# Hybrid decoder layer in f32: one h sum from two f32 tiles, small columns behind x's scaling, w_o's second operand in halves, the last rows' residual in PSUM

## The chip, the cores and the metric

The kernel runs on one core of one Trainium2 chip. The metric is the time of one execution on the device in microseconds (us); lower is better. A core has TensorE (matmuls; PE in the profile, PEld for its weight loads), VectorE (DVE), ScalarE (ACT), GpSimd (POOL) and SyncE (SP), which issues most DMAs. They run side by side and meet through semaphores. Matmul results land in PSUM, everything else lies in SBUF.

## The reference

One decoder layer on 512 tokens of width 1024, all in f32. Cut to what matters:

```
h = rmsnorm(x, attn_norm_g)
u_b, u_c, u_x, q, k, v, g_conv, g_attn = split(h @ w_in)
y_conv = (u_b * short_conv(u_c * u_x, conv_w)) @ w_conv_out
y_attn = sliding_window_attention(q, k, v, sinks, rel_bias) @ w_attn_out
x = x + (sigmoid(g_conv) * y_conv + sigmoid(g_attn) * y_attn) @ w_o
h2 = rmsnorm(x, mlp_norm_g)
x = x + square(relu(h2 @ w_up)) @ w_down
return rmsnorm(x, final_norm_g)
```

## The kernel before

**Precision.** Every f32 operand is split into a high part (ScalarE rounds it to fp32r) and a low part (VectorE subtracts the high part from the f32 value). A product is three passes of matmuls, called kinds in the code: high by high, low by high, high by low. So each product needs a ScalarE copy before its first pass and a VectorE subtraction before each of the others.

**Fast products.** The q projection and the 13 stages GC, GA, CO, AO, WO and eight stages of w_up and w_down use a Strassen scheme of seven products of 2 x 2 blocks: M1, N2, M6, M5, M7, M3, N4, in this order. Their left operands are corners of the activations or sums of corners (S1 to S4), their right ones weight blocks or sums of weight blocks (T1 to T4). Results of several products add up in the same PSUM region, and ScalarE copies or VectorE sums take them out between products.

**Front.** SP loads x in four blocks of 128 rows between halves of the first q weights. For each block ScalarE takes the sum of squares and a root (`root(b)`, lines 1221 to 1228), VectorE takes its reciprocal and scales the block (`scale_x`, lines 1749 to 1754), and TensorE transposes it (`x_transposes`). Behind the second block's transposes come four idle transposes and product M1. The gain columns `pcol` come from a transpose of `prow`; VectorE copies them out of PSUM (line 1797). With them VectorE and ScalarE take each transposed tile into `h`, split in high and low (`tile_high`, `tile_low`). ScalarE also writes the second half's tiles unsplit into `qa` (`tile_whole`, counted by `wide`). These are the corners A21 and A22; the corner A11 exists only as high and low parts in `h`.

**h sums of the q product.** VectorE makes S3 = A11 - A21 (`h_s3`, two steps), S2 = -A22 - S3 (`h_s2`), S1 = A11 + S2 (`h_s1`, two steps: A11's high part, then its low part) and S4 = A12 + S2 (`h_s4`, two steps). `hs_step` counts the steps. `sum_high` and `sum_low` split each sum; they feed M7, M6, M5 and M3 of the q product. In VectorE's order, `h_s1` stands directly ahead of `q_low_part(M6)`, the low part of M6's weights, which M6's third pass waits for.

**Mixer.** Behind the q product come k and v's heads and four blocks of conv strips (c, x, b) with attention between them. The first scores (TensorE, lines 811 and 812) need `qs`, which VectorE finishes only when the table `bias` has landed (line 2057 waits for it, and `stage_queries` follows).

**Stage WO.** Here `mixed` is the left operand. Product M1 has transposes of the last corner of `mixed` between its matmuls (`mixed_corner_21`); `s_high(WO, N2)` copies that corner's high part straight from PSUM (line 1472), `s_low` the low part. N2 adds to a copy of M1's result (`seed_out`, counted by `o_seeded`), one half of rows each.

**End.** In the last stage `res` holds the residual. VectorE drains products into it (`drain`, `drain_last_m3`, `drain_n4`). N4 runs row block by row block (`by_blocks`), three passes each; `drain_n4(12, 1)` adds the last one, rows 3, columns 0 to 511. ScalarE sums the squares of each row block in two halves, takes the root (`root_of`), VectorE the reciprocal (`factor`) and scales one half (`scale_late`), ScalarE the other (`scale_early`); SP and ScalarE store.

Of the kernel before, what the change touches and what calls it, by code (L numbers as in the profile page):

```python
# [9 lines left out]
ALU = mybir.AluOpType  # L10
# [201 lines left out]
def build(nc, x, attn_norm_g, w_in, conv_w, w_conv_out, attn_sinks, rel_bias, w_attn_out, w_o,  # L212
          mlp_norm_g, w_up, w_down, final_norm_g, out):
    ctx = ExitStack()
    with ctx:
# [132 lines left out]
        def sem(name):  # L348
            return ctx.enter_context(nc.semaphore(name))
# [41 lines left out]
        m_hi, m_lo, t_sum = sem("m_hi"), sem("m_lo"), sem("t_sum")  # L391
        t1_base, t1_in, t3_base, t3_in = sem("t1_base"), sem("t1_in"), sem("t3_base"), sem("t3_in")
        copied, half_copied = sem("copied"), sem("half_copied")
        o_seeded = sem("o_seeded")
        summed, relu_done = sem("summed"), sem("relu_done")
        squared, s_sum, s_hi, s_lo = sem("squared"), sem("s_sum"), sem("s_hi"), sem("s_lo")
        ao_sum = sem("ao_sum")
        prod, drained, gfin_in = sem("prod"), sem("drained"), sem("gfin_in")
        passed = sem("passed")
        root_done, root3_part, root3_done = sem("root_done"), sem("root3_part"), sem("root3_done")  # L400
        ss3_ready, fin_step = sem("ss3_ready"), sem("fin_step")
# [367 lines left out]
        def _(pe):  # L769
# [282 lines left out]
            def product(s, i, fresh, between={}):  # L1052

                n, thi, tlo = weight_parts(s, i)
                if s < CO:
                    shi, slo = gate_part(i)
                else:
                    shi, slo = s_hi_tile[slot_of(s, i)], s_lo_tile[slot_of(s, i)]
                parts = [(shi, thi), (slo, thi), (shi, tlo)]
                order = [(b, kind) for b in range(2) for kind in range(3)] if by_blocks(s, i) else \  # L1060
                    [(b, kind) for kind in range(3) for b in range(2)]
                if seeded(s) and i == N2:
                    order = [(0, 0), (0, 1), (1, 0), (1, 1), (0, 2), (1, 2)]
                for at_, (b, kind) in enumerate(order):
                    if n == 0 and kind == 0:
                        pe.wait_ge(free_dve[b], frees("D", b, S_OUT - 1))
                    if s == WO and i == N2 and kind == 0:
                        pe.wait_ge(o_seeded, b + 1)
                    if seeded(s) and i == N2 and kind == 0:
                        pe.wait_ge(copied, copied_no(s, 1)) if b else pe.wait_ge(half_copied, s)  # L1070
                    if b == 0:
                        if kind == 0:
                            pe.wait_ge(m_hi, n + 1)
                            if s >= CO:
                                pe.wait_ge(s_hi, part_no(s, i) + 1)
                            elif i in HS:
                                pe.wait_ge(hs_in[HS.index(i)], 32)
                        elif kind == 1:
                            if s >= CO:
                                pe.wait_ge(s_lo, part_no(s, i) + 1)  # L1080
                        else:
                            pe.wait_ge(m_lo, n + 1)
                    a_, w = parts[kind]
                    for k in range(4):
                        last = mm(pair[region(s, i)][:, b, :], a_[:, k, b * P:(b + 1) * P], w[:, k, :],  # L1085
                                  start=(fresh and kind == 0 and k == 0), stop=(kind == 2 and k == 3),
                                  skip_group_check=True)
                    if kind == 2:
                        last.then_inc(prod, 1)
                    if at_ in between:  # L1090
                        between[at_]()
# [25 lines left out]
            for s in range(STAGES):  # L1117
# [65 lines left out]
                pe.wait_ge(drained, base_ + 3 + more)  # L1183
                product(s, M3, False)
                pe.wait_ge(drained, base_ + 4 + more)
                if s == WO:
                    pe.wait_ge(h2_raw, 4)
                    residual_transposes(1, 1, 0)
# [4 lines left out]
        def _(act):  # L1193
# [84 lines left out]
            root(1)  # L1278
            q_high_half(M1, 0)
            q_high_half(M1, 1)  # L1280
            act.wait_ge(par_ready, 1)
            for k in range(4, 8):
                act.wait_ge(h_ready, k - 3)
                tile_high(0, k, k)
            root(2)
            q_high_half(N2, 0)
            q_high_half(N2, 1)
            root(3)
# [10 lines left out]

            def sum_high(i):  # L1300

                act.wait_ge(hs_step, {M7: 2, M6: 3, M5: 5, M3: 7}[i])
                k = HS.index(i)
                a(hs_hi[k][:, :, :], hs_sum[k][:, :, :], ACT.Copy).then_inc(hs_split, 1)

            def q_copy(i, j, of, done, scale=1.0):

                act.wait_ge(q_prod, 2 * Q_ORDER.index(of) + 2)
                if i:
                    act.wait_ge(hs_step, 3)  # L1310
                a(four_of(qa, i, j), four(Q_REGION.get(of, 3))[:, :, :], ACT.Copy, scale=scale).then_inc(done, 1)

            q_copy(0, 0, M1, q_c11_base)
# [141 lines left out]
            def s_high(s, i):  # L1455

                at_ = part_no(s, i)
                if i in (M1, N2, N4):
                    if s == CO:
                        for j in range(2):  # L1460
                            act.wait_ge(free_dve[j], frees("D", j, S_OUT - 1))
                    elif s == AO:
                        act.wait_ge(pv_out, QUADS * TB)
                    elif s == WO:
                        act.wait_ge(mix_t, 4) if i == N2 else act.wait_ge(mix_ready, {M1: 2, N4: 1}[i])
                    else:
                        act.wait_ge(squared, 4 * ((s - 6) // 2) + {M1: 1, N4: 2, N2: 3}[i])
                else:
                    act.wait_ge(sums(s), sums_before(s) + {M7: 1, M6: 2, M5: 3, M3: 4}[i])
                wait_used(act, *part_before(s, i))  # L1470
                src = four(0) if (s, i) == (WO, N2) else part_source(s, i)
                a(s_hi_tile[slot_of(s, i)][:, :, :], src[:, :, :], ACT.Copy).then_inc(s_hi, 1)  # L1472

            def seed(s):

# [130 lines left out]
            def square(s, at_):  # L1606
# [3 lines left out]
                    act.wait_ge(s_lo, part_no(s - 1, N4) + 1)  # L1610
                a(a_part(s, i, j), src[:, :, :], ACT.Square).then_inc(squared, 1)

            def sum_squares(b, ch, part):
                a(tz[:, 0, 0:512], res[:, b, 512 * ch:512 * ch + 512], ACT.Square,
                  accum_out=ss3[:, part, b:b + 1]).then_inc(ss3_ready, 1)

            def early_squares(b):
# [87 lines left out]
            act.wait_ge(root3_part, 1)  # L1705

            def root_of(b):
                act.wait_ge(drained, drained_before(STAGES - 1) + 6 + b)
                act.wait_ge(ss3_ready, TB + b)
                sum_squares(b, 1 - early(b), 1)  # L1710
                act.wait_ge(ss3_ready, TB + b + 1)
                a(rms3[:, 1, b:b + 1], ss3[:, 1, b:b + 1], ACT.Sqrt, bias=rms3[:, 0, b:b + 1],
                  scale=1.0 / D).then_inc(root3_done, 1)
# [23 lines left out]
        def _(dve):  # L1737
# [55 lines left out]
                    tile_low(1, at_, LATE_TILES[at_])  # L1793

            scale_x(0)
            dve.wait_ge(par_t, 1)
            v.tensor_copy(pcol[:, :], bank[KT - 1][:, T - 5 * KT:T]).then_inc(par_ready, 1)
            scale_x(1)
            dve.wait_ge(par_ready, 1)
            for k in range(4):  # L1800
                tile_high(k)
# [34 lines left out]
                                       op0=ALU.mult, op1=ALU.subtract).then_inc(hs_step, 1)  # L1836

            def h_s1():
                step_done(3)
                v.tensor_tensor(hs_sum[2][:, :, :], h_part(0, 0, 0), hs_sum[1][:, :, :], ALU.add).then_inc(hs_step, 1)  # L1840
                step_done(4)
                v.tensor_tensor(hs_sum[2][:, :, :], hs_sum[2][:, :, :], h_part(1, 0, 0), ALU.add).then_inc(hs_step, 1)

            def h_s4():
                step_done(3)
                v.tensor_tensor(hs_sum[3][:, :, :], h_part(0, 0, 1), hs_sum[1][:, :, :], ALU.add).then_inc(hs_step, 1)
                step_done(6)
                v.tensor_tensor(hs_sum[3][:, :, :], hs_sum[3][:, :, :], h_part(1, 0, 1), ALU.add).then_inc(hs_step, 1)

            def sum_low(i):  # L1850
# [266 lines left out]
            def drain_n4(s, b):  # L2117
# [4 lines left out]
                r = res[:, 2 + b, 0:512]  # L2122
                v.tensor_tensor(r, r, pair[region(s, N4)][:, b, :], ALU.add).then_inc(drained, 1)

            def drain_last_m3(b):

                s = STAGES - 1
                dve.wait_ge(prod, 14 * s + 2 * M3 + b + 1)
                dve.wait_ge(drained, drained_before(s) + 5 + b)
                r = res[:, b, 512:D]  # L2130
                v.tensor_tensor(r, r, pair[region(s, M3)][:, b, :], ALU.add).then_inc(drained, 1)
# [239 lines left out]
            def scale_late(b):  # L2371

                dve.wait_ge(fin_step, b + 1)
                ch = 1 - early(b)
                r = res[:, b, 512 * ch:512 * ch + 512]
                v.scalar_tensor_tensor(out=r, in0=r, scalar=rms3[:, 2, b:b + 1], in1=gfin[:, 512 * ch:512 * ch + 512],
                                       op0=ALU.mult, op1=ALU.mult).then_inc(out_late, 1)

            for s in range(WO + 1, STAGES, 2):
# [42 lines left out]
                low_part(s + 1, M3)  # L2422
                drain(s + 1, 3 + more, 1, 1, M7, ALU.subtract)
                if last:
                    drain_last_m3(0)
                s_low(s + 1, N4)
                low_part(s + 1, N4)
# [13 lines left out]
            factor(1)  # L2441
            scale_late(1)
            gain(3)
            drain_n4(STAGES - 1, 1)
            factor(2)
            scale_late(2)
            dve.wait_ge(gained_late, 1)
# [25 lines left out]
```

## Time and profile before

| | us |
|---|---|
| median of 3 runs | 751.18 (751.17 to 751.3) |
| the profiled execution | 751.2 |
| its span | 749.5 |
| TensorE busy | 741.1 (99%), 4198 matmuls |
| VectorE busy | 656.3 (88%) |
| ScalarE busy | 430.0 (57%) |
| GpSimd busy | 85.5 (11%) |
| granted TensorE clock, mean | 0.999 |

The span is what the profiler's rows cover; the 1.7 us around it belong to the time too. A row of the timeline is one instruction or a run of like ones: start, time, engine, line, operation, written tile <- read tiles, shapes, count, and in brackets how long the engine had been idle and what ended that. Matmuls overlap, and their ends are modelled, so two products are compared by starts.

### The profile page before, as it was taken

To read this page: it belongs to the slowest core of one execution; us is meant where nothing else is said; L and a number is where in the kernel's file an instruction comes from. 1 tells how busy PE (TensorE), PEld (TensorE's weight loads), DVE (VectorE), ACT (ScalarE), POOL (GpSimd) and SP (SyncE) were. 2 spreads that over 40 slices of the span, in tenths; PEclk is the share of its full clock that TensorE was granted. 3 is DMA by queue.
4 is the path that set the end of the run, shared out by engine and by line. 5 is a ranking of instruction groups with operands and counts; after the bars stand their busy time and mean duration, and the time that the engine had idled before them with its cause. 6 is when DMAs were issued, how large, how long until landed. Compare 5 with 4: busy or idle time off the path is not lost.

```text
span 749.5 us, 10670 instructions
## 1 busy us (share of the span) xinstructions
PE 741.1 (99%) x4198; PEld 650.7 (87%) x4198; DVE 656.3 (88%) x759; ACT 430.0 (57%) x551; POOL 85.5 (11%) x120
## 2 busy tenths in 40 slices
PE   9999999999999999999999999999999999999996
PEld 8899888888888888888888899889988999899985
DVE  5996788989899686989999999998799879986997
ACT  6773555453644557564658776654565455545555
POOL 1520000111122101010100101010101010100102
PEclk9999999999999999999999999999999999999999
DMA  9899313161247987777767747677677767686703
GB/s 319 200 316 321 112 57 113 57 164 61 84 127 236 305 232 196 195 225 193 255 169 177 213 124 208 179 201 193 169 191 202 174 171 219 168 215 180 197 1 113
DMA packets 69443, 135.45 MB, mean 181 GB/s; under 512 B 2636, under 2 KB 18068, under 8 KB 69396
## 3 DMA queue, kind: packets, MB, share of 16 engines
q1 hardware_dynamic: 48848, 85.23, 33.6%
q0 software_dynamic: 20336, 49.30, 30.3%
q8 instruction: 32, 0.52, 0.3%
q10 hardware_dynamic: 212, 0.28, 0.1%
q14 instruction: 15, 0.12, 0.1%
HBM read 128.48 MB, written 6.32 MB: 180 GB/s over the span
## 4 chain that ended last, share of the span: by engine, by line
PE 94%; DVE 4%; ACT 1%; issue 1%; POOL 0%; POOLq 0%; DVEq 0%; ACTq 0%
PE pair L1085 45%; PE pair L1044 22%; PE pair L790 6%; PE pair L792 6%; PE pair L791 6%; PE pair L911 3%; PE pair L837 2%; PE pair L812 1%; PE pair L811 1%; PE pair L821 1%; PE pair L859 1%; DVE h L1788 1%; PE pair L1007 0%; PE pair L995 0%; DVE wgt L1745 0%
## 5 line engine op out<-in xcount | busy, mean ns | idle before, releaser
L1390 ACT ACTIVATE high<-home_raw 128x2048 fp32r<-128x2048 f32 x91 | 174.3, 1916 | 148.4 <-PE pair L1085 102.9
L2014 DVE TENSOR_TENSOR home_lo<-home_raw,high 128x2048 fp32r<-128x2048 f32 x91 | 208.4, 2290 | 34.6 <-ACT high L1390 34.1
L1085 PE MATMUL pair<-high,s_hi_tile 128*128 128x512 f32 x440 | 110.3, 391 | 0.3 <-ACT s_hi_tile L1472 0.3
L1085 PE MATMUL pair<-high,s_lo_tile 128*128 128x512 f32 x440 | 109.9, 390 | 0.0
L1085 PE MATMUL pair<-home_lo,s_hi_tile 128*128 128x512 f32 x440 | 109.5, 389 | 0.0
L1085 PEld LDWEIGHTS pair<-home_lo,s_hi_tile 128*128 128x128 f32 x440 | 82.5, 188 | 17.1
L1085 PEld LDWEIGHTS pair<-high,s_lo_tile 128*128 128x128 f32 x440 | 82.4, 188 | 17.1
L1085 PEld LDWEIGHTS pair<-high,s_hi_tile 128*128 128x128 f32 x440 | 81.8, 188 | 17.7 <-issue 0.7
L790 PE MATMUL pair<-h,wgt 128*128 128x512 f32 x192 | 76.5, 399 | 0.0
L792 PE MATMUL pair<-h,wgt 128*128 128x512 f32 x192 | 75.0, 390 | 0.0
L791 PE MATMUL pair<-h,wgt 128*128 128x512 f32 x192 | 74.9, 390 | 0.0
L1044 PE MATMUL pair<-h_hi,home_lo 128*128 128x256 f32 x448 | 58.4, 283 | 0.0
L1044 PE MATMUL pair<-h_lo,high 128*128 128x256 f32 x448 | 58.4, 283 | 0.0
L1044 PE MATMUL pair<-h_hi,high 128*128 128x256 f32 x448 | 58.3, 283 | 0.0
L1044 PEld LDWEIGHTS pair<-h_hi,high 128*128 128x128 f32 x448 | 56.0, 192 | 0.3
L1044 PEld LDWEIGHTS pair<-h_hi,home_lo 128*128 128x128 f32 x448 | 55.8, 192 | 0.0
L1044 PEld LDWEIGHTS pair<-h_lo,high 128*128 128x128 f32 x448 | 55.8, 192 | 0.0
L792 PEld LDWEIGHTS pair<-h,wgt 128*128 128x128 f32 x192 | 36.0, 188 | 7.9
L791 PEld LDWEIGHTS pair<-h,wgt 128*128 128x128 f32 x192 | 36.2, 188 | 6.6
L790 PEld LDWEIGHTS pair<-h,wgt 128*128 128x128 f32 x192 | 36.1, 188 | 6.7
L1362 ACT ACTIVATE pr<-pr,neg_m 128x128 f32<-128x128 f32 x64 | 24.8, 390 | 26.1 <-DVE pr L1930 22.8
L1745 DVE TENSOR_TENSOR wgt<-raw,wgt 128x1024 fp32r<-128x1024 f32 x26 | 30.8, 1221 | 6.5 <-ACT wgt L1211 6.4
(228 smaller groups left out, 1129.5 us busy)
## 6 DMA issues: line engine op xcount, KB each, us to landing
home_raw<-in_w_up SPq DMA_DIRECT2D x16, 1024.0 KB, 5.3
home_raw<-in_w_down SPq DMA_DIRECT2D x16, 1024.0 KB, 5.1
raw<-in_w_in SPq DMA_DIRECT2D x26, 512.0 KB, 4.8
home_raw<-in_w_up POOLq DMA_DIRECT2D x12, 1024.0 KB, 8.2
home_raw<-in_w_down POOLq DMA_DIRECT2D x12, 1024.0 KB, 8.4
home_raw<-in_w_in POOLq DMA_DIRECT2D x7, 1024.0 KB, 8.6
home_raw<-in_w_in SPq DMA_DIRECT2D x7, 1024.0 KB, 7.1
home_raw<-in_w_conv_out SPq DMA_DIRECT2D x4, 1024.0 KB, 5.2
```

What stands on the lines that cost most here:

```text
L790: mm(bank[j][:, :], wh, rhs[:, 0, k, :], start=(k == 0), stop=False)
L791: mm(bank[j][:, :], wh, rhs[:, 1, k, :], start=False, stop=False)
L792: last = mm(bank[j][:, :], wl, rhs[:, 0, k, :], start=False, stop=(k == KT - 1))
L811: mm(acc, q, khi[:, kg, keys], start=True, stop=False)
L837: last = mm(bank[B_PV][:, :], vs[:, kb, kg, :, :].rearrange("p a d -> p (a d)"), pt[:, part, kb, :], start=(e == 0), stop=(e == len(steps) ...
L911: last = mm(acc[:, f, :], w[:, k, f * P:(f + 1) * P], a_[:, k, :], start=(i in (M1, N2, M5) and kind == 0 and k == 0 and f % 2 == 0), stop ...
L1044: last = mm(acc[:, f, :], w[:, k, f * P:(f + 1) * P], a_[:, k, :], start=(fresh and kind == 0 and k == 0 and f % 2 == 0), stop=(kind == 2 ...
L1085: last = mm(pair[region(s, i)][:, b, :], a_[:, k, b * P:(b + 1) * P], w[:, k, :], start=(fresh and kind == 0 and k == 0), stop=(kind == 2 ...
L1362: a(v, v, ACT.Exp, bias=neg_m[:, qd % 2, i:i + 1], accum_out=den[:, qd % 2, i:i + 1])
L1390: a(high[n % 2][:, :], home_raw[home_of(s, name)][:, :], ACT.Copy).then_inc(m_hi, 1)
L1745: v.tensor_tensor(w[:, 1, 1024 * e:1024 * e + 1024], raw[raw_slot(2 * s1 + e)][:, :], f32(w[:, 0, 1024 * e:1024 * e + 1024]), ALU.subtract ...
L2014: v.tensor_tensor(home_lo[home][:, :], home_raw[home][:, :], f32(high[n % 2][:, :]), ALU.subtract).then_inc(m_lo, 1)
```

## The change

- The h sum S1 is made in one step, A21 - A22, from the two unsplit tiles in `qa`; the steps that follow count one less, and the q copies that overwrite these tiles wait for it.
- VectorE copies `pcol` behind the second block's scaling rather than ahead of it. ScalarE takes the third block's root ahead of its four tile copies rather than behind them.
- In stage WO the high part of N2's second operand is copied in two halves; TensorE waits for the first (`o_first`) ahead of the product and for the second ahead of its third matmul.
- In the last stage VectorE adds the residual of rows 3, columns 0 to 511, into the PSUM bank ahead of N4 (`add_residual`, new, behind the drain of M7); N4's second row block adds up on it. Its drain is dropped, and ScalarE's squares and VectorE's final scaling of these rows read PSUM. TensorE waits for the new sum (`rested`) ahead of N4.

The diff, cut:

```diff
@@ product
-                            if s >= CO:
+                            if s == WO and i == N2:
+                                pe.wait_ge(o_first, 1)
+                            elif s >= CO:
                                 pe.wait_ge(s_hi, part_no(s, i) + 1)
...
                     for k in range(4):
+                        if s == WO and i == N2 and (b, kind, k) == (0, 0, 2):
+                            pe.wait_ge(s_hi, part_no(s, i) + 1)
@@ TensorE, stage order
                 pe.wait_ge(drained, base_ + 4 + more)
+                if s == STAGES - 1:
+                    pe.wait_ge(rested, 1)
@@ ScalarE, front
             q_high_half(M1, 1)
+            root(2)
             act.wait_ge(par_ready, 1)
             for k in range(4, 8):
                 act.wait_ge(h_ready, k - 3)
                 tile_high(0, k, k)
-            root(2)
@@ sum_high, q_copy
-                act.wait_ge(hs_step, {M7: 2, M6: 3, M5: 5, M3: 7}[i])
+                act.wait_ge(hs_step, {M7: 2, M6: 3, M5: 4, M3: 6}[i])
...
                 if i:
-                    act.wait_ge(hs_step, 3)
+                    act.wait_ge(hs_step, 4)
@@ s_high
-                src = four(0) if (s, i) == (WO, N2) else part_source(s, i)
-                a(s_hi_tile[slot_of(s, i)][:, :, :], src[:, :, :], ACT.Copy).then_inc(s_hi, 1)
+                src, first = four(0) if (s, i) == (WO, N2) else part_source(s, i), 0
+                if (s, i) == (WO, N2):
+                    first = 2
+                    a(s_hi_tile[slot_of(s, i)][:, 0:2, :], src[:, 0:2, :], ACT.Copy).then_inc(o_first, 1)
+                a(s_hi_tile[slot_of(s, i)][:, first:4, :], src[:, first:4, :], ACT.Copy).then_inc(s_hi, 1)
@@ sum_squares, root_of
+            def last_rows(b, ch):
+
+                return pair[region(STAGES - 1, N4)][:, 1, :] if (b, ch) == (3, 0) else res[:, b, 512 * ch:512 * ch + 512]
...
-                a(tz[:, 0, 0:512], res[:, b, 512 * ch:512 * ch + 512], ACT.Square,
+                src = last_rows(b, ch) if part else res[:, b, 512 * ch:512 * ch + 512]
+                a(tz[:, 0, 0:512], src, ACT.Square,
...
-                act.wait_ge(drained, drained_before(STAGES - 1) + 6 + b)
+                if b < 3:
+                    act.wait_ge(drained, drained_before(STAGES - 1) + 6 + b)
+                else:
+                    wait_used(act, STAGES - 1, N4)
@@ VectorE, front
             scale_x(0)
+            scale_x(1)
             dve.wait_ge(par_t, 1)
             v.tensor_copy(pcol[:, :], bank[KT - 1][:, T - 5 * KT:T]).then_inc(par_ready, 1)
-            scale_x(1)
@@ h_s1, h_s4
             def h_s1():
-                step_done(3)
-                v.tensor_tensor(hs_sum[2][:, :, :], h_part(0, 0, 0), hs_sum[1][:, :, :], ALU.add).then_inc(hs_step, 1)
-                step_done(4)
-                v.tensor_tensor(hs_sum[2][:, :, :], hs_sum[2][:, :, :], h_part(1, 0, 0), ALU.add).then_inc(hs_step, 1)
+                v.tensor_tensor(hs_sum[2][:, :, :], four_of(qa, 1, 0), four_of(qa, 1, 1), ALU.subtract).then_inc(hs_step, 1)
...
-                step_done(6)
+                step_done(5)
@@ VectorE, end
+            def add_residual():
+
+                s = STAGES - 1
+                dve.wait_ge(drained, drained_before(s) + 5)
+                acc = pair[region(s, N4)][:, 1, :]
+                v.tensor_tensor(acc, acc, res[:, 3, 0:512], ALU.add).then_inc(rested, 1)
...
-                v.scalar_tensor_tensor(out=r, in0=r, scalar=rms3[:, 2, b:b + 1], in1=gfin[:, 512 * ch:512 * ch + 512],
+                src = pair[region(STAGES - 1, N4)][:, 1, :] if b == 3 else r
+                v.scalar_tensor_tensor(out=r, in0=src, scalar=rms3[:, 2, b:b + 1], in1=gfin[:, 512 * ch:512 * ch + 512],
...
                 if last:
+                    add_residual()
                     drain_last_m3(0)
...
             gain(3)
-            drain_n4(STAGES - 1, 1)
             factor(2)
```

## Rows read from the trace of the kernel before

**Rows 1.** The page's first part: busy us, share, instructions of each engine.

```profile
PE 741.1 (99%) x4198; PEld 650.7 (87%) x4198; DVE 656.3 (88%) x759; ACT 430.0 (57%) x551; POOL 85.5 (11%) x120
```

**Rows 2.** The list of waits, TensorE alone: waiter <- releaser: total us, times, longest.

```profile
PE pair L911 <- DVE q_lo L1768: 0.2, 1, 0.2
```

**Rows 3.** Timeline, second block of x: start, us, engine, line, operation [idle before].

```profile
7.12 0.29 ACT L1227 ACTIVATE rms<-ssq,eps 128x1 f32<-128x1 f32 x1
...
7.46 0.20 DVE L1797 COPY pcol<-pair 128x40 f32<-128x40 f32 x1 [0.42 <-PE pair L864]
...
9.12 1.66 DVE L1776 TENSOR_SCALAR h<-pair,pcol 128x256 fp32r<-128x256 f32 x4 [0.61 <-PE pair L851]
```

**Rows 4.** Timeline, third and fourth block; then x's loads there, issue and landing.

```profile
11.27 1.60 ACT L1264 ACTIVATE h<-pair,pcol 128x256 fp32r<-128x256 f32 x4 [0.76 <-issue]
...
13.93 0.30 ACT L1227 ACTIVATE rms<-ssq,eps 128x1 f32<-128x1 f32 x1
...
17.52 0.17 DVE L1752 RECIPROCAL rms<-rms 128x1 f32<-128x1 f32 x1 [0.47 <-ACT rms L1227]
...
L542 SPq DMA_DIRECT2D xn<-in_x x2: 442/537/632, 2.8 to 3.5; - x2
...
DMA to landing us min/median/max: 7.8/8.1/8.4
```

**Rows 5.** Timeline, products M6, M5 and M7 of q and VectorE's h sum.

```profile
34.41 2.08 PE L911 MATMUL pair<-hs_hi,q_hi 128*128 128x256 f32 x16
...
35.14 1.22 DVE L1842 TENSOR_TENSOR hs_sum<-hs_sum,h 128x1024 f32<-128x1024 f32 x1
36.28 2.28 DVE L1768 TENSOR_TENSOR q_lo<-q_raw,q_hi 128x2048 fp32r<-128x2048 f32 x1
...
37.80 2.01 ACT L1241 ACTIVATE q_hi<-q_raw 128x1024 fp32r<-128x1024 f32 x2 [0.34 <-DMA q_raw<-in_w_in]
...
40.63 2.08 PE L911 MATMUL pair<-hs_hi,q_hi 128*128 128x256 f32 x16
...
46.39 2.08 PE L911 MATMUL pair<-hs_hi,q_hi 128*128 128x256 f32 x16
```

**Rows 6.** A stretch (busy us per engine; last: clock, DMA share, GB/s); timeline, first scores.

```profile
32.00:72.00 40.00, 39.78 (x291) 37.80 (x290) 33.21 (x27) 21.30 (x21) 6.41 (x10) 1.00 1.06 325
...
68.48 0.56 DVE L2057 TENSOR_TENSOR vdif<-vnat 128x384 f32<-128x384 f32 x1 [6.10 <-DMA bias<-bias_rows]
...
69.07 2.47 DVE L1903 TENSOR_TENSOR qs<-qa,qs 64x1024 fp32r<-64x1024 f32 x2
...
72.05 0.19 PEld L811 LDWEIGHTS pair<-khi,qs 128*128 128x128 f32 x1
```

**Rows 7.** Timeline, stage WO from M1's end to N2's third pass.

```profile
391.56 1.03 ACT L1472 ACTIVATE s_hi_tile<-pair 128x1024 fp32r<-128x1024 f32 x1 [0.29 <-PE pair L1007]
...
392.62 1.23 DVE L2070 TENSOR_TENSOR s_lo_tile<-pair,s_hi_tile 128x1024 fp32r<-128x1024 f32 x1 [0.18 <-ACT s_hi_tile L1472]
392.70 1.69 PEld L1085 LDWEIGHTS pair<-high,s_hi_tile 128*128 128x128 f32 x8 [0.68 <-issue]
...
393.76 2.28 DVE L2014 TENSOR_TENSOR home_lo<-home_raw,high 128x2048 fp32r<-128x2048 f32 x1
...
396.25 1.77 PEld L1085 LDWEIGHTS pair<-home_lo,s_hi_tile 128*128 128x128 f32 x8
396.47 1.98 PE L1085 MATMUL pair<-home_lo,s_hi_tile 128*128 128x512 f32 x8
```

**Rows 8.** Timeline of VectorE in the last stage's end.

```profile
735.19 0.69 DVE L2131 TENSOR_TENSOR res<-res,pair 128x512 f32<-128x512 f32 x1 [0.50 <-PE pair L1085]
...
742.80 0.68 DVE L2369 TENSOR_TENSOR res<-res,gfin 128x512 f32<-128x512 f32 x1
743.40 0.68 DVE L2123 TENSOR_TENSOR res<-res,pair 128x512 f32<-128x512 f32 x1
...
745.25 0.15 DVE L2362 RECIPROCAL rms<-rms 128x1 f32<-128x1 f32 x1
```

More of the change, by code:

```diff
@@ L393, in build @@
         copied, half_copied = sem("copied"), sem("half_copied")
-        o_seeded = sem("o_seeded")
+        o_seeded, o_first = sem("o_seeded"), sem("o_first")
         summed, relu_done = sem("summed"), sem("relu_done")
@@ L397, in build @@
         ao_sum = sem("ao_sum")
-        prod, drained, gfin_in = sem("prod"), sem("drained"), sem("gfin_in")
+        prod, drained, rested, gfin_in = sem("prod"), sem("drained"), sem("rested"), sem("gfin_in")
         passed = sem("passed")
```

## The prediction, made before the change was run

> **What bounds the kernel now.** I read the page first: the TensorE row is busy for 741.1 of 749.5 us [rows 1], so time is won only where TensorE stands still, has not begun, or has already ended. The list of waits by engine, TensorE alone, has three entries: the start, one on q_lo of 0.2 us [rows 2], and one on s_hi_tile, met again in edit 3. That list counts from a matmul's modelled end, so I measured both stalls again from starts in the timeline. The reader is to look for three places: the front up to 72 us, where VectorE and ScalarE feed TensorE just in time; the passage inside stage WO at 392 us; and the last 6 us, where no matmul runs and VectorE and ScalarE work by turns. The edits lie in these places, two in the first, one each in the others. From 72 to 735 us the kernel runs at TensorE's pace: loads wait for its progress (`wait_used`), so a gain in front should shift all behind it, unless something there stands at a fixed time. One thing does: the table `bias`.
>
> **Edit 1, the small columns behind x's scaling.** ScalarE's root of the second block ends at 7.41, but VectorE copies pcol first (7.46, 0.20 us) [rows 3] and begins the scaling's reciprocal behind it, some 0.08 before the copy's end (such overlaps below), at 7.58. Without the copy ahead it can start at about 7.46: 0.12 us earlier. The scaling, x's second transposes, four idle transposes and product M1 follow in a row, so TensorE has the 0.12. The copy moves into VectorE's wait of 0.61 us for these transposes [rows 3]; without that cover it would cost its 0.20 again.
> root(2) goes ahead of the four tile copies. ScalarE is idle for 0.76 us before them, from 10.51 to 11.27 [rows 4]. x's third block is issued at 2.8 and takes at least 7.8 us [rows 4], so it lands at 10.6, and the root, which in before stands behind the copies (from 12.78 to 14.23), then runs from 10.65 to 12.1. The price: tiles 4 to 7 come 0.8 us later, where nobody is near: VectorE takes them up behind the third block's scaling, TensorE with product N2. root(3) ends up to 0.45 earlier, and VectorE's wait of 0.47 for it at 17.52 [rows 4] goes. But what TensorE waits for there, the transposes of x's fourth block, isn't in its list at all, so it is below 0.1: I take 0.06 (0 to 0.1). Sum of edit 1: 0.18 us (0.12 to 0.22). If the q copies behind find their load not yet landed, the 0.06 goes and the 0.12 stays.
>
> **Edit 2, one h sum.** Two sums of 1.22 us become one, whose inputs VectorE has already waited for. Product M6 takes 40.63 - 34.41 = 6.22 us from its first matmul to M5's first; M5, with the same 48 matmuls, takes 46.39 - 40.63 = 5.76 [rows 5]: the stall on q_lo is 0.46. q_lo ends at 38.56; without one sum (1.22 and a gap of 0.04) at 37.3, with edit 1 at 37.1, and TensorE asks for it 0.46 before it gets it now, at 38.1. The stall goes whole: 0.46. Next late: M5's q_hi, which waits for a transfer and is ready at 39.81 [rows 5], independent of the edit; M5 begins at 39.99 and needs its second half a quarter pass later. The q copies now wait for four steps instead of three; the fourth ends before 35.2, the first copy that heeds it follows M5, so that wait is free.
>
> **Where the front's gain can be lost.** The two edits bring TensorE to the first scores 0.64 us earlier. There it needs qs: VectorE starts vdif at 68.48, when the table `bias` has landed, and ends the two halves of qs at 71.54; the scores' first load is at 72.05 [rows 6]. With 0.04 for the signal the slack is 0.47, not 0.64. The table's load stands behind q's products on SP's queue and is issued earlier too; does it land earlier? From 32 to 72 us the DMA share is 1.06 at 325 GB/s [rows 6], that is, the engines are full: I take the same landing, 0.01 off for what comes with it, hence 0.46. Bounds: 0.66 if the table moves along, 0.2 if it lands 0.27 later, since POOL's T3 block, which starts when the h sums are stored, comes earlier as well and shares the engines.
> The Trainium skill, DMA: Bandwidth & Descriptors, section Issuing engines are not separate DMA queues, says that transfers of all issuing engines run on the same 16 engines and interleave, whoever started them. By that rule the early issue is worth nothing and the front gives 0.46; with a table that moves with its issue, 0.64. No row of before shows it by itself.
>
> **Edit 3, w_o's second operand in halves.** ScalarE copies s_hi in 1.03 us from 391.56. TensorE's load for N2 comes at 392.70, behind an idle 0.68 [rows 7]: that is the stall. In the steady flow a load runs 0.22 ahead of its matmul (396.25 and 396.47), so a part of a load's lateness doesn't show; I take 0.11 of the 0.22. With a first half of about 0.6 us, done at 392.16, the load comes at 392.25 and 0.45 or more of the stall goes. But two halves end about 0.08 later than one copy (a fixed part twice). VectorE's s_low waits for the second (392.62, 1.23 us) and low_part follows without a gap (393.76, 2.28 us) to 396.05; N2's third pass loads at 396.25 [rows 7]. That slack of 0.20, less 0.05 for the signal and the 0.08, plus the hidden 0.11, is all that TensorE keeps: 0.18 us. seed_out(1) and ScalarE's work behind it are 0.08 later, which M6, the next product, doesn't see: its loads come after N2's third pass. Bounds: 0 (the halves cost 0.25 more) and 0.3.
>
> **Edit 4, the residual in PSUM.** Behind the last matmul VectorE adds the last rows at 743.40 (0.68 us); the reciprocal for these rows is at 745.25 [rows 8]. The add goes, and ScalarE squares PSUM directly. VectorE starts an instruction 0.60 after such an add (743.40 behind 742.80), so its queue is 0.60 shorter. ScalarE's part, 745.25 - 744.08 = 1.17 us with both signals, then starts with the last matmul's end (743.34) and is done at 744.5: it binds no longer, VectorE's queue does. Against this, add_residual is new in that queue, ahead of drain_last_m3(0), which waited 0.50 for TensorE until 735.19 [rows 8]. It can start at 734.73, takes 0.69 like the drain of the same size, and the drain may follow at 735.33: 0.14 late, with s_low, low_part and all of VectorE's tail. N4's third pass waits for that low_part, so TensorE ends up to 0.14 later, 744.65 for ScalarE's part, still ahead of VectorE. The reciprocal comes at 745.25 - 0.60 + 0.14 = 744.79: 0.46 us, and the stores behind it with it. TensorE's new wait on `rested` (done at 735.4) is for N4, behind the whole of M3: free, 0.14 if not. Bounds: 0.25 (the add from and to PSUM takes 0.9) and 0.6 (it hides in the 0.50).
> The final scaling now reads PSUM. A sum with one operand in PSUM (743.40) and one from SBUF alone (742.80) both take 0.68 us [rows 8]: no difference, as I take it. The Trainium skill, VectorE: DVE Perf Modes, section The TRN2 errata, gives a PSUM source 62 cycles more; by that estimate, 0.065 us, edit 4 would give 0.40.
>
> **Sum.** 0.46 + 0.18 + 0.46 = 1.10 us. The profiled execution took 751.2 us, of which 749.5 are its span; the median of the runs is 751.18, so the sum needs no correction: 750.1 us. All bounds on the good side give 0.66 + 0.3 + 0.6 = 1.56: 749.6; on the bad side 0.2 + 0 + 0.25 = 0.45: 750.75.
>
> **Rivals.** (a) The table moves with its issue, the halves cost nothing and the new add hides: about 1.5 us, 749.6. For it: VectorE's work ahead of these transfers is earlier by up to 1.4 us. Against: the full DMA engines.
> (b) Only the end gains: the front is given back at the scores or the next weights, and stage WO's gain behind low_part: 0.4 us, 750.8. For it: slacks of 0.47 and 0.20.
> (c) Slower: the table lands much later, because the T3 block of 1 MB gets ahead of it. Each microsecond by which it lands later takes one from the 1.1; it decides from 69.6 on. At 325 GB/s the block is 3.2 us; that half of it is served first would be 1.6 later, 751.7. Against: both are in the queues as it is, and the work up to the landing stays the same.
> (d) The PSUM sum doesn't spare its instruction, as when N4 waits for `rested`: bounded in edit 4.
>
> **How the numbers follow.** A measurement of this kernel can tell about 0.2%, 1.5 us, from no change. Forecast (749.75 to 750.65): 0.66; (a) 0.17; (b) 0.12; (c) 0.05. Faster by over 0.2% (under 749.68) is (a) and a little of the forecast's good end, 0.18; slower by over 0.2% lies past (c)'s price, 0.02; within is the rest, 0.80. The range takes the forecast, (a)'s near half and (b): 749.5 to 750.85.
>
> **What would show it.** Right: no TensorE wait on q_lo; M5's first matmul at 39.99; vdif still at about 68.5 and the scores' first load near 71.6, not 71.4; N2's third pass bound by low_part; the last reciprocal directly behind the other blocks' work on VectorE. Wrong: vdif at 67.9 (a) or past 69 (c), a TensorE wait on `rested`, or a new wait between 72 and 735 us that takes back what the front gave.

## The result and the profile after

The changed kernel takes 754.52 us (median of 7 executions, 752.93 to 756.97) where the kernel before takes 751.18 (750.95 to 751.5): a ratio of 1.0041, 95% interval 1.0031 to 1.0052. The forecast was 750.1, its range ended at 750.85. So the change makes the kernel slower, by more than the 0.2% that such a measurement can tell, and it makes the seven executions differ by 4 us where the seven of the kernel before differed by half a microsecond (in larger sets of that kernel single ones took up to 752.92). The profiled execution took 755.13 us, of which 753.4 are its span: 3.9 more than before.

The page's first part, the row that answers to [rows 1], and behind it two rows from the list of waits of TensorE in the first 80 us (waiter <- releaser: total us, times, longest), which answers to [rows 2]:

```profile
PE 742.4 (99%) x4198; PEld 651.5 (86%) x4198; DVE 655.2 (87%) x758; ACT 429.9 (57%) x552; POOL 85.0 (11%) x120
```

```profile
PE pair L911 <- ACT hs_hi L1310: 2.3, 1, 2.3
...
PE pair L911 <- ACT q_hi L1247: 0.9, 1, 0.9
```

The wait on q_lo is gone, as forecast. These two have come, both at q's products (L911). The timeline of M6 and M5, which answers to [rows 5], shows that the front's gain arrived and where it was lost (start, us, engine, line, operation, [idle before <- releaser]):

```profile
34.13 2.08 PE L911 MATMUL pair<-hs_hi,q_hi 128*128 128x256 f32 x16
36.05 2.08 PE L911 MATMUL pair<-hs_lo,q_hi 128*128 128x256 f32 x16
37.97 2.08 PE L911 MATMUL pair<-hs_hi,q_lo 128*128 128x256 f32 x16
40.92 1.34 PE L911 MATMUL pair<-hs_hi,q_hi 128*128 128x256 f32 x9 [0.87 <-ACT q_hi L1247]
...
52.73 0.63 PE L952 MATMUL pair<-ident,ty 128*128 128x128 f32 x4
...
55.61 1.69 PE L911 MATMUL pair<-hs_hi,q_hi 128*128 128x256 f32 x11 [2.26 <-ACT hs_hi L1310]
```

M6's third pass starts at 37.97, 0.65 earlier than the 38.62 of the trace before: the 0.64 of edits 1 and 2 is there in this pair of executions. Then M5 begins at 40.92, where it began at 40.63 [rows 5], and M3 at 55.61, where it began at 52.50. The rows of the trace before for these comparisons, and of ScalarE's copy of M3's load:

```profile
38.62 2.17 PE L911 MATMUL pair<-hs_hi,q_lo 128*128 128x256 f32 x16 [0.22 <-DVE q_lo L1768]
...
47.51 1.90 ACT L1256 ACTIVATE q_hi<-q_raw 128x2048 fp32r<-128x2048 f32 x1
...
52.50 2.15 PE L911 MATMUL pair<-hs_hi,q_hi 128*128 128x256 f32 x16
```

What ScalarE waited for ahead of these, and what GpSimd and SyncE's queue issued there, stands in the timeline of the changed kernel:

```profile
37.33 1.32 POOL L673 DMA_DIRECT2D q_raw<-in_w_in  x1 [2.21 <-DVE q_lo L1785]
38.46 0.75 POOL L699 DMA_DIRECT2D h_sums<-hs_hi  x1
39.00 0.74 POOL L699 DMA_DIRECT2D h_sums<-hs_lo  x1
39.81 2.00 ACT L1247 ACTIVATE q_hi<-q_raw 128x1024 fp32r<-128x1024 f32 x2 [3.89 <-DMA q_raw<-in_w_in]
39.88 0.37 SPq L549 DMA_DIRECT2D q_raw<-in_w_in  x1
...
52.61 1.91 ACT L1262 ACTIVATE q_hi<-q_raw 128x2048 fp32r<-128x2048 f32 x1 [4.61 <-DMA q_raw<-in_w_in]
54.43 1.04 ACT L1310 ACTIVATE hs_hi<-hs_sum 128x1024 fp32r<-128x1024 f32 x1
```

L673 at 37.33 is GpSimd's accumulating transfer of 1 MB for N4 (`add_q(N4)`), which waits for q_lo of M6. L549 at 39.88 is SyncE's load of 1 MB for M3 (`load_q(M3)`, semaphore q_b22), which waits for the landing of M5's accumulation (q_t1_in). In the trace before they stand the other way round:

```profile
37.87 0.37 SPq L549 DMA_DIRECT2D q_raw<-in_w_in  x1
38.86 1.32 POOL L673 DMA_DIRECT2D q_raw<-in_w_in  x1 [3.48 <-DVE q_lo L1768]
```

Before, M3's load took 7.1 us from issue to landing (45.0) and ScalarE took it up without a wait at 47.51. After, it took 12.7 (52.6); ScalarE stood idle for 4.61 us for it, and hs_hi, which TensorE names, is only the next instruction in ScalarE's queue. The chain of work that ended last (start, us, what) says it in three lines: M5's base load, M5's accumulation, M3's load, one behind the other.

```profile
19.39 10.49 DMA q_raw<-in_w_in
30.17 9.61 DMA q_raw<-in_w_in
39.88 12.71 DMA q_raw<-in_w_in
```

The third part of the loss is the clock. Stretches of 4 us of the changed kernel (busy us by engine; the last three columns are granted clock, DMA share, GB/s):

```profile
48.00:52.00 4.00, 4.00 (x36) 4.00 (x35) 3.92 (x6) 0.00 (x1) 0.00 (x0) 1.00 1.04 416
52.00:56.00 4.00, 1.71 (x13) 1.33 (x13) 1.08 (x2) 3.39 (x3) 0.00 (x0) 1.00 1.04 393
56.00:60.00 4.00, 4.00 (x24) 4.00 (x23) 3.97 (x3) 3.27 (x3) 1.06 (x2) 0.61 1.10 363
60.00:64.00 4.00, 4.00 (x35) 4.00 (x33) 3.79 (x4) 0.00 (x0) 0.00 (x0) 0.97 1.07 398
```

From 56.9 to 60.3, beginning 1.3 us after TensorE took up work again, the matmuls of M3 follow each other every 0.213 us instead of 0.120: the engine was granted 1.2 GHz instead of 2.4, which makes the mean of the third stretch 0.61.

The whole account, from the start of the same matmul in both traces (after minus before): -0.65 at M6's third pass, +0.29 at M5's first matmul, +0.58 at the transposes in front of M3, +3.11 at M3's first matmul, +4.60 where the clock is full again, +4.59 at the first scores, and +3.92 at VectorE's last reciprocal. So the front lost 0.94 before M5, 0.29 up to the transposes, 2.53 before M3 and 1.49 to the clock, and the edits behind it gave back 0.67.

### The profile page after: what moved, and what is told of

The parts are those of the page before. It is cut to its first block, busy times and chain, and to the rows that moved or that the text cites. A ratio compares the mean times of both kernels' runs of the same rounds, so it can differ in the third digit from the quotient of the medians.

```text
span 753.4 us, 10670 instructions
## 1 busy us (share of the span) xinstructions
PE 742.4 (99%) x4198; PEld 651.5 (86%) x4198; DVE 655.2 (87%) x758; ACT 429.9 (57%) x552; POOL 85.0 (11%) x120
## 4 chain that ended last, share of the span: by engine, by line
PE 87%; DMA 5%; DVE 4%; issue 2%; ACT 1%; ACTq 0%; SPq 0%; DVEq 0%
PE pair L1089 41%; PE pair L1044 20%; PE pair L790 6%; PE pair L792 6%; PE pair L791 6%; DMA q_raw<-in_w_in 4%; PE pair L911 3%; PE pair L837 2%; DVE home_lo L2028 2%; PE pair L812 1%; PE pair L811 1%; PE pair L821 1%; DVE res L2129 1%; ACT high L1396 1%; DMA xn<-in_x 0%
```

## Experiments

Three theories were set against each other. A: q's transfers. It has two forms: A1, M3's load is passed by N4's accumulation, because edit 2 brings GpSimd's issue forward; A2, M5's accumulation is late by itself, because edit 1 brings its base load forward. B: the order of instructions on ScalarE and VectorE. C: the end edits. The four parts come first, each against the kernel before.

**Edits 1 and 2 alone** (the diff's hunks for `root(2)`, `scale_x`/`pcol`, `h_s1` and its step numbers).

> Only edits 1 and 2 (x's scaling and root order, one h sum); stage WO and the tail as before. Theory A (q's transfers): the whole loss sits here, in M5's wait for q_t1_in (0.9 us) and M3's wait for q_b22 (2.5 us) with the low clock behind it (1.5 us); so 753.5 to 757.5 us, that is 0.6 to 0.7 above the full change, with the same run-to-run spread of some 4 us, and the load of q_b22 landing at about 52 instead of 45. Theory B (the order on ScalarE and VectorE, not the transfers, makes the waits): the waits on hs_hi and q_hi stand with the loads landing long before the copies begin. Theory C (the end edits cost it): 750.5 to 751.0 and no new wait.

754.08 us (750.52 to 756.3); ratio 1.0031, 1.0014 to 1.0047. In its trace N4's accumulation is issued at 37.43, M3's load at 39.43; it lands 13.0 us later, and TensorE waits 2.5 us before M3. The copies begin when their load lands, within 0.1 us. C and B fall. Two details of A's expectation were missed: the wait before M5 was 0.3 us instead of 0.9, and the time isn't 0.6 to 0.7 above the full change's but 0.44 below it, in a kernel whose executions differ by 5.8 us. Three of its 12 executions took 750.5 to 750.65, some 0.65 less than before, the forecast's gain of the front; no trace shows one of them.

**Edit 1 alone.**

> Only edit 1 (pcol's copy behind x's scaling, root(2) ahead of the tile copies). N4's accumulation is issued behind q_lo of M6, so with edit 1 alone still at about 38.6, after or with q_b22's load (37.9 or later). Theory A1 (N4's accumulation passing q_b22's load is the cause): q_b22 lands by 47 and M3 doesn't wait; 751.0 to 751.6. Theory A2 (the base load of M5, issued 0.27 us earlier against M7's accumulation, is the cause): q_t1_base lands near 29.9, q_t1_in past 38.7, q_b22 after 48, TensorE waits for both; 752.5 or more, with a wide spread.

751.35 us (750.81 to 753.28), ratio 1.0006, 0.9997 to 1.0015: no loss that can be told, and no gain. N4's accumulation goes out at 38.70, M3's load at 39.10, and it lands 6.4 us later. q_t1_base landed at 29.53 and q_t1_in at 39.01, but TensorE didn't wait for it. By the median, A2's 752.5 didn't come. But five of the 11 executions took 752.67 to 753.28, where five of the 35 of the kernel before took 752.18 or more; no trace shows one of them, so what they waited for stays open.

**Edit 2 alone.**

> Only edit 2 (h_s1 in one sum). q_lo of M6 ends 1.26 earlier, so N4's accumulation is issued at about 37.6 instead of 38.87. Theory A1: q_b22 lands late (49 or more), TensorE waits 1 to 3 us before M3 and its clock falls behind it; 752.5 to 756. Theory A2: q_t1_base lands at 29.1 as before, q_t1_in near 37.8, q_b22 near 45; 750.7 to 751.0, the forecast's gain of 0.46.

754.91 us (750.65 to 757.51), ratio 1.004, 1.0022 to 1.0058. The loss comes with this edit alone, the one that only takes work away.

```profile
38.32 1.32 POOL L673 DMA_DIRECT2D q_raw<-in_w_in  x1 [2.21 <-DVE q_lo L1768]
39.65 0.37 SPq L549 DMA_DIRECT2D q_raw<-in_w_in  x1
```

In these rows of its timeline SyncE issues in the moment in which GpSimd's issue ends, and M3's load already takes 12.3 us to its landing. TensorE waits 1.9 us before M3.

**Edits 3 and 4 alone.**

> Only edits 3 and 4 (w_o's operand in halves, residual in PSUM); the front as before. Theory of the forecast: 0.18 + 0.46 = 0.64 faster, 750.5 us, spread as of before (0.5). The rival that the halves or the PSUM sum cost something: 751.2 or more. By the changed kernel's trace (shift of TensorE's last matmul against the shift before stage WO, and of the last reciprocal): 0.68.

750.67 us against 751.25, ratio 0.9995, 0.9987 to 1.0004: the 0.58 lies near the 0.64 of the sum, in an interval that takes in no change as well. Nothing is lost there.

The next two test the order itself, from both sides.

**The full change, N4's accumulation held back.**

```
 pool.wait_ge(q_low, 5)
+pool.wait_ge(q_t1_in, 16)
 add_q(N4, 1, 0, q_t4_in)
```

> The full change, with one wait more: GpSimd issues N4's accumulation only when q_t1_in has landed, as SyncE does with q_b22's load, so that SyncE's short issue (0.37 us) comes ahead of GpSimd's (1.3 us). Theory A1 (the order of these two transfers is the whole loss): q_b22 lands 6 to 8 us after its issue, at 45 to 47, no wait before M3, the front keeps its 0.46 to 0.66 and the kernel takes 750.0 to 750.4, the time that was forecast. Theory A2 (M5's accumulation is late by itself, since its base load is issued earlier beside M7's): q_t1_in at 38.5 to 39.8 all the same, 0.3 to 0.9 us of wait before M5 stay; 750.5 to 751.3, and more where the clock falls behind that wait.

750.23 us (749.8 to 751.13) against 751.26: ratio 0.9988, 0.9979 to 0.9997. One wait more on an engine that is 11% busy takes 4.3 us off the changed kernel's time, and the sum of the forecast, 750.1, is met within 0.13. Rows of its timeline, and then the last line of the view of L549, its time from issue to landing:

```profile
39.41 0.37 SPq L549 DMA_DIRECT2D q_raw<-in_w_in  x1
39.89 1.32 POOL L673 DMA_DIRECT2D q_raw<-in_w_in  x1 [4.55 <-DMA q_raw<-in_w_in]
...
40.45 0.74 PE L912 MATMUL pair<-hs_hi,q_hi 128*128 128x256 f32 x4 [0.19 <-ACT q_hi L1248]
```

```profile
DMA to landing us min/median/max: 5.6/5.6/5.6
```

M3's load lands after 5.6 us, at 45.0 as before, and N4's accumulation, now behind it, takes 14.1 (54.0) without a stall of TensorE. A wait before M5 is left (0.2 in this execution, which took 750.64), since q_t1_in landed at 39.32: A2's landing came, the time that it asked for didn't.

**The same without edit 1.**

> As the kernel before it, but with edit 1 undone (edits 2, 3, 4 and N4's accumulation held for q_t1_in). Theory A1: 750.2 to 750.5, as the one with edit 1 or up to 0.2 above. Theory A2: the base load of M5 is issued at 19.7 again and q_t1_in lands at 37.8 to 38.2; no wait before M5, so faster than with edit 1, 750.1 to 750.3 against 750.5 to 751.3.

750.28 us (749.99 to 751.3), ratio 0.9988, 0.9979 to 0.9997. A2 wanted M5's wait to go: it didn't, q_t1_in landed at 39.96 in the profiled execution (751.3, the slowest of the 11) and TensorE waited 0.7. So M5's accumulation can be late without edit 1, and edit 1 brings nothing here that can be told (0.05).

**The kernel before, with the two transfers in the reverse order.**

```
...
 add_q(N4, 1, 0, q_t4_in)
+pool.wait_ge(bias_out, 16)
+g.memset(ext[:, 0:1], NEG).then_inc(n4_out, 1)
...
+sp.wait_ge(n4_out, 1)
 load_q(M3, 1, 1, q_b22)
```

> The kernel before, every instruction as it was, but q_b22's load is issued only when GpSimd has issued N4's accumulation (a one-column fill on GpSimd behind the issue tells SyncE): at about 40.3 instead of 37.87. Theory A1: q_b22 lands at 50 to 53, though its issue is only 2.4 us later; TensorE waits 1 to 3 us before M3, 752.5 to 756, with a wide spread. Rival (the load is late by its issue alone, 45.0 + 2.4 = 47.4; ScalarE takes it up at 47.5): no wait, 751.2.

756.21 us (755.81 to 757.91), ratio 1.0066, 1.0052 to 1.008. None of the edits is in this kernel, and it has the loss, in every execution. First two rows of its timeline, then the time of L549 from issue to landing, then the first line of the list of waits. The profiled execution is the slowest of the five (757.91).

```profile
39.19 1.32 POOL L674 DMA_DIRECT2D q_raw<-in_w_in  x1 [3.47 <-DVE q_lo L1771]
40.63 0.37 SPq L549 DMA_DIRECT2D q_raw<-in_w_in  x1
```

```profile
DMA to landing us min/median/max: 13.4/13.4/13.4
```

```profile
PE pair L914 <- ACT hs_hi L1307: 4.0, 1, 4.0
```

The load is issued 2.8 us later than before and lands 9.0 us later (54.04 against 45.01). A1 stands, though it came out dearer than expected (a wait of 4.0 us for 1 to 3, and a time 0.2 over the 756); the rival's 47.4 doesn't.

**Edit 3 alone.**

> Only edit 3 (w_o's second operand in halves). The forecast: 0.18, so 751.0; by the changed kernel's trace N2's third pass begins 0.32 earlier, so up to 0.32, 750.85, if nothing gives it back behind. Rival: given back in the next products, 751.2. Edit 4 is the difference to the run with both (750.67).

751.11 us against 751.26, ratio 1.0, 0.9991 to 1.0009. The 0.15 lies near the forecast's 0.18, but no run resolves it.

**The full change, M3's load set free from q_t1_in.** The other way to put it ahead of N4's accumulation.

```
-sp.wait_ge(q_t1_in, 16)
 load_q(M3, 1, 1, q_b22)
```

> The full change, but SyncE doesn't wait for q_t1_in before q_b22's load: it is issued behind bias_rows, at about 30.1 instead of 39.9, at the same time as M5's accumulation (30.2, 1.3 us of issue on GpSimd). Theory A1 (whichever of two 1 MB transfers is issued first is served first): q_b22 lands by 36, M3 never waits, but M5's accumulation comes behind it: q_t1_in at 41.5 to 43 instead of 39.8, TensorE waits 1.5 to 3 us before M5; 751.5 to 754. Rival (the idle time of the DMA engines between 28 and 32 us, where their share is 0.34, takes the load in): q_t1_in at 39.8 or little later, at most 1 us of wait before M5; 750.0 to 750.8, as good as holding N4's accumulation back.

752.35 us (750.18 to 754.17), ratio 1.0015, 1.0006 to 1.0024. Again the transfer issued first is served first, only that the victim is now M5's accumulation: M3's load (29.70) lands in 5.5 us, M5's accumulation, issued 0.11 behind it, takes 11.5 instead of 9.6 and lands at 41.27 (expected: 41.5 to 43). Its timeline, then the first line of its list of waits:

```profile
29.70 0.37 SPq L549 DMA_DIRECT2D q_raw<-in_w_in  x1
29.81 1.29 POOL L672 DMA_DIRECT2D q_raw<-in_w_in  x1 [3.48 <-DMA q_raw<-in_w_in]
```

```profile
PE pair L910 <- ACT q_hi L1246: 2.3, 1, 2.3
```

The share of 0.34 that the DMA engines show between 28 and 32 us in the changed kernel didn't take 1 MB more in without making the accumulation behind it late.

All ten traces with both transfers at this place, sorted by the time that M3's load took:

| kernel | N4's issue, start to end | M3's load issued | its time to landing |
|---|---|---|---|
| full, N4 held, no edit 1 | 40.53 to 41.85 | 40.05 | 5.4 |
| full, N4 held | 39.89 to 41.21 | 39.41 | 5.6 |
| edit 1 | 38.70 to 40.02 | 39.10 | 6.4 |
| edit 3 | 38.74 to 40.07 | 38.83 | 6.9 |
| before | 38.86 to 40.19 | 37.87 | 7.1 |
| edits 3 and 4 | 38.93 to 40.25 | 38.04 | 7.2 |
| edit 2 | 38.32 to 39.65 | 39.65 | 12.3 |
| full change | 37.33 to 38.65 | 39.88 | 12.7 |
| edits 1 and 2 | 37.43 to 38.76 | 39.43 | 13.0 |
| before, reversed | 39.19 to 40.51 | 40.63 | 13.4 |

In the first six rows SyncE's load is issued before GpSimd's issue of 1.32 us has ended, in the last four when it has. Where between the two the border lies isn't measured: the latest load of the first group went out 0.40 us after the start of GpSimd's issue, the earliest of the second 1.33 us after it.

## Why the prediction was wrong, point by point

**Edit 2, "Next late: M5's q_hi, which waits for a transfer and is ready at 39.81, independent of the edit".** This is the step that failed, twice. First, M5's q_hi is not the dearest of what comes late next. q_lo of M6, which the edit moves forward by 1.26 us, has a second reader beside TensorE: GpSimd waits for it with `add_q(N4)`. The forecast followed the earlier q_lo to TensorE alone. One look at who waits for q_lo would have shown 1 MB set off 1.3 us earlier, which in the trace before was issued only 1.0 us behind M3's load. The term that this cost, a late M3 at 2.53 us and the lower clock behind it at 1.49, isn't in the sum at all. Second, "independent of the edit" took a landing of one execution for a fixed time. In the traces of the five kernels without edit 2's sum q_t1_in landed at 37.78, 37.95, 38.74, 39.01 and 39.01. The trace before is the earliest of these; the slack of a microsecond that hid the others was just what the 0.64 of the front was to consume. In the six with it, N4 held back or not, q_t1_in landed at 39.32 to 41.27. The loss needs both: with N4's issue 1.3 us earlier (37.6 to 38.9) and M3's load still at 37.87, the load would have been issued before GpSimd's issue had ended, as in the table's first group; in the three kernels with edit 2 and the loss it was issued only at 39.43 to 39.88, behind q_t1_in. What makes that transfer late is told only for the run in which M3's load was set free. For the rest it stays open: already q_t3_base, issued and landed before any instruction that edit 2 touches, came at 17.88 to 18.40 in the six and at 17.14 to 17.85 in the five.

**"The stall goes whole: 0.46", edit 1's 0.18.** Right up to 37.97 (0.65 for 0.64). Of the 0.65, 0.28 is there at M6's first matmul (34.13 for 34.41) and 0.37 comes inside M6. The second part is firm: from M6's first matmul to its third pass it is 3.83 or 3.84 us in all six traces with edit 2 and 4.16 to 4.21 in the five without, and with edit 2 alone M6 takes 5.75 us instead of 6.22. The first is edit 1's 0.18 mixed with what two executions differ by: M6 begins at 34.13 to 34.35 in the five traces with edit 1 and at 34.34 to 35.13 in the six without. Whether edit 1's part reaches the end wasn't resolved by any run.

**"Where the front's gain can be lost".** The right question at the wrong transfer. The forecast looked for a transfer that is passed by another and took the table `bias`, the one thing whose landing stood in TensorE's way at 72 us. The table wasn't it: it landed earlier, not later, with vdif at 66.73 in the changed kernel and at 67.57 with N4 held, against 68.48 [rows 6].

```profile
66.73 0.56 DVE L2071 TENSOR_TENSOR vdif<-vnat 128x384 f32<-128x384 f32 x1
...
76.64 0.19 PEld L811 LDWEIGHTS pair<-khi,qs 128*128 128x128 f32 x1
```

So the "same landing" was wrong too, on the good side; the cut from 0.64 to 0.46 wasn't put to the test by the changed kernel, whose first scores come at 76.64 for other reasons. The Trainium skill, DMA: Bandwidth & Descriptors, section Issuing engines are not separate DMA queues, has transfers of all engines interleave on the same 16. The traces agree once packets of both queues are moving (205 of GpSimd's queue and 197 of SyncE's from 45 to 48 us in the changed kernel); before that, the transfer issued later waits for its first packet, and so M3's load takes 5.4 to 7.2 us when it is issued first and 12.3 to 13.4 when GpSimd's megabyte has been issued, while N4's accumulation takes 10.0 to 11.7 in front and 12.3 to 14.2 behind (packets in the last section).

**Rival (c)**, with a chance of 0.05, had the mechanism, a transfer that gets ahead of another, and the sign. It was tied to `bias` and priced at 1.6 us by bandwidth alone. It left out that a late operand costs TensorE twice: 2.5 us of wait, and 1.49 at the lower clock behind it. In other traces a wait of 1.9 us (edit 2), 2.3 (M3's load set free) or 4.0 (the reversed order) was followed by stretches of 4 us at 0.70, 0.78 and 0.50 as well; in that of edits 1 and 2, a wait of 2.5 us was followed by none, with 1.00 from 52 to 64 us. So the clock's part comes or doesn't. The mean clock of the changed kernel's executions fits this as one source of their spread (0.999 in the two fastest, 752.93 and 753.40; 0.995 in two of the three slowest, 755.13 and 756.97); the landing itself is likely another, but only one of the seven has a trace.

**The signs.** None of the signs of being wrong that the prediction lists names this place: it looked for a new wait from 72 us on, and both came before 56. One of its signs of being right does, M5's first matmul at 39.99, and that one failed (40.92). Its sign for a faster kernel, vdif at 67.9, was more than met (66.73) in a slower one.

**Edit 3.** The mechanism is right. The rows that answer to [rows 7]:

```profile
396.16 0.60 ACT L1480 ACTIVATE s_hi_tile<-pair 128x512 fp32r<-128x512 f32 x1 [0.29 <-PE pair L1007]
396.65 0.59 ACT L1481 ACTIVATE s_hi_tile<-pair 128x512 fp32r<-128x512 f32 x1
396.87 0.77 PEld L1089 LDWEIGHTS pair<-high,s_hi_tile 128*128 128x128 f32 x4 [0.25 <-issue]
...
398.42 2.28 DVE L2028 TENSOR_TENSOR home_lo<-home_raw,high 128x2048 fp32r<-128x2048 f32 x1
...
400.75 1.24 PEld L1089 LDWEIGHTS pair<-home_lo,s_hi_tile 128*128 128x128 f32 x6 [0.37 <-DVE home_lo L2028]
```

TensorE's idle time ahead of N2's load falls from 0.68 to 0.25, so 0.43 of the stall goes (forecast 0.45); low_part ends at 400.70 and then binds the third pass, as the forecast said. Of the 0.43, 0.16 is left where N2 ends (forecast 0.18).

**Edit 4.** The new sum, and the last reciprocals and scaling, which answer to [rows 8]:

```profile
739.17 0.70 DVE L2144 TENSOR_TENSOR pair<-pair,res 128x512 f32<-128x512 f32 x1
...
747.91 0.16 DVE L2383 RECIPROCAL rms<-rms 128x1 f32<-128x1 f32 x1
...
749.17 0.15 DVE L2383 RECIPROCAL rms<-rms 128x1 f32<-128x1 f32 x1
749.36 0.75 DVE L2398 SCALAR_TENSOR_TENSOR res<-pair,rms,gfin 128x512 f32<-128x512 f32 x1
```

From TensorE's last matmul (742.95 before, 747.41 after) to the last reciprocal it is 1.76 us instead of 2.31: 0.55, where the forecast had 0.46 (0.60 less 0.14 for the new sum in VectorE's queue). The new sum took 0.70 (forecast 0.69) and let the drain behind it come 0.14 later, but TensorE's last matmul isn't later for it. The scaling from PSUM took 0.75 as it did from SBUF, so the 0.065 us by which the prediction's other estimate made it dearer doesn't show.

**The sum.** With the two transfers in their old order the same four edits give 751.26 - 750.23 = 1.03 for the forecast's 1.10. That the total comes so close is in part luck, since each of these differences has an interval of some 0.7 us to either side. The end edits alone gave 0.58 (forecast 0.64), which leaves 0.45 for the front (0.46); but no trace shows the front's 0.46 arrive. In the one with N4 held, one of that kernel's slower executions, M6's third pass is 0.43 ahead of the trace before, M5 0.18 ahead, M3 0.14 behind, and the first scores come at 72.19 against 72.05 [rows 6]. So the medians contradict no term of the sum; what was missing was a term.

## What to carry to other kernels

When an instruction is moved forward, list everyone who waits for it, not only the one whose stall it is to remove; a GpSimd or SyncE that issues a transfer on it can put a megabyte ahead of a load that is needed sooner. Where DMA engines are full, the order of issue between two queues is part of the schedule, and if it rests on chance it should be written down as a wait: here one `wait_ge` on an idle engine turned 754.5 us into 750.2. A landing read from one execution is a sample; before it serves as slack, compare several traces: it was q_t1_in's landing that decided whether the earlier accumulation got ahead.

## What was not expected of the hardware

Of two transfers of 1 MB from different queues, the one issued first had the DMA engines nearly to itself at first, and then the two shared them. For SyncE's load, issue before or after the end of GpSimd's 1.32 us was the difference between 5.4 to 7.2 and 12.3 to 13.4 us, with nothing between. A GpSimd issue that had begun 0.40 us earlier (38.70 against 39.10, edit 1) didn't get ahead. The packets by queue (packets, MB, and the time that they took as a share of the 16 engines' time, which can pass 100%; q0 is GpSimd's queue, q1 SyncE's) show how: first the trace before from 40 to 43 us, then the changed kernel from 40 to 43, then from 45 to 48:

```profile
q1 hardware_dynamic: 352, 0.71, 91.0%
q0 software_dynamic: 7, 0.02, 4.3%
```

```profile
q0 software_dynamic: 280, 0.67, 105.6%
```

```profile
q0 software_dynamic: 205, 0.49, 68.8%
q1 hardware_dynamic: 197, 0.40, 39.6%
```

Before, M3's load runs almost alone. In the changed kernel GpSimd's queue, the tail of two stores and then N4's accumulation, runs alone; the load's first packet starts at 43.7, 3.8 us after its issue, and then the two queues move about as many packets each, of which GpSimd's take more of the engines' time (68.8% against 39.6%). In the six traces of the first group the load's first packet starts 1.0 to 1.4 us after the issue, in the four of the second 3.4 to 3.8. So some 2.5 of the 5.6 us by which the load takes longer in the changed kernel than before are a late start; the rest falls into the time of sharing. The first transfer is an accumulation, and whether a plain one in its place would hold the load up as long wasn't tried. Nor were GpSimd's two stores of 0.5 MB, which stand behind the accumulation in its queue, moved without it; in the changed kernel they land after it (50.8 and 52.8 against 49.0).

Not settled: what moves M5's accumulation between 8.4 and 9.6 us from issue to landing when no other megabyte is in front, and why single executions of the kernel before, too, took up to 752.92 us. Of 77 executions of that kernel beside the experiments seven took 752.18 or more; of the 22 with N4 held none took more than 751.3. That fits an order of the two transfers that chance decides in the kernel before as well, but none of the seven has a trace.
